# Attention in eight places per pair: a head group's last turn and products of values moved into the next pair

## What is computed

```python
proj = h @ w_in
# A: 8 query heads over 2 key/value heads, head_dim 64, dense; q and k RMS-normalised, 2-D rotary
s = jnp.einsum('bqgrd,bkgd->bgrqk', q_blk, k)
p = jax.nn.softmax(s, axis=-1)
a_o = jnp.einsum('bgrqk,bkgd->bqgrd', p, v)
# B: three groups of 8 heads, (window, dilation) = (128,1), (512,4), (2048,16), partial rotary
o, lse = _dilated_group(_partial_rope(b_q, pos) * scale, _partial_rope(b_k, pos), b_v, window, dilation)
wts = jax.nn.softmax(jnp.stack(lses, axis=0), axis=0)
b_o = jnp.einsum('gbsh,gbshd->bshd', wts, jnp.stack(outs, axis=0))
x = x + jnp.concatenate([a_o, b_o], axis=-1) @ w_out
# then: RMSNorm -> SwiGLU FFN -> residual; the second layer's mixer is a gated recurrence
```

## Time and profile before

| | us |
|---|---|
| median of 3 runs | 1305.33 |
| lowest, highest | 1304.08, 1308.48 |
| profiled execution, its own time | 1305.52 |
| its span in the trace | 1303.7 |

### The profile page before, as it was taken

How to read it: one execution, slowest core, us unless ns; L and a number is a source line. 1 busy time by engine, 2 the same in 40 slices (tenths; PEclk the granted TensorE clock), 3 DMA queues, 4 the chain that set the end, 5 groups by cost and what they waited for, 6 DMA issues and landing times.

```text
span 1303.7 us, 18386 instructions
## 1 busy us (share of the span) xinstructions
PE 1285.2 (99%) x6525; PEld 1030.1 (79%) x6525; DVE 560.3 (43%) x872; ACT 551.6 (42%) x1006; POOL 611.3 (47%) x487
## 2 busy tenths in 40 slices
PE   8999999999999999999999999999999999999998
PEld 7877777777778888888888876777888888888886
DVE  4866575756644512222202026999843131311011
ACT  5454444444434433333323246786433333333233
POOL 4565564646535444444444543530244444444442
PEclk9999999999999999999999999999999999999999
DMA  6422222222314333333332353214333333333332
GB/s 217 150 73 62 68 64 59 57 66 67 120 56 115 91 97 97 97 97 97 98 97 88 105 166 117 81 57 145 91 97 96 98 95 98 96 116 98 96 98 94
DMA packets 123415, 126.31 MB, mean 97 GB/s; under 512 B 7896, under 2 KB 106456, under 8 KB 122712
## 3 DMA queue, kind: packets, MB, share of 16 engines
q1 hardware_dynamic: 123320, 125.46, 32.1%
q10 hardware_dynamic: 32, 0.01, 0.0%
HBM read 119.15 MB, written 6.29 MB: 96 GB/s over the span
## 4 chain that ended last, share of the span: by engine, by line
PE 58%; issue 21%; POOL 12%; DVE 5%; ACT 3%; POOLq 0%; DMA 0%; SPq 0%; ACTq 0%; DVEq 0%
PE ps L1495 17%; PE ps L1497 16%; PE ps L1496 16%; POOL w_lo L495 11%; PE ps L1855 2%; PE ps L1613 1%; PE ps L1648 1%; PE ps L1625 1%; PE ps L1629 1%; PE ps L1590 1%; POOL rot L504 1%; PE ps L1659 1%; PE ps L1667 1%; DVE bkn L1139 1%; ACT w_hi L555 0%
## 5 line engine op out<-in xcount | busy, mean ns | idle before, releaser
L495 POOL TENSOR_TENSOR w_lo<-w_stage,w_hi 128x512 fp32r<-128x512 f32 (+2 forms) x430 | 543.3, 1268 | 676.8 <-ACT w_hi L555 676.4
L555 ACT ACTIVATE w_hi<-w_stage 128x512 fp32r<-128x512 f32 (+2 forms) x448 | 264.0, 594 | 582.4 <-PE ps L1497 570.0
L1495 PE MATMUL ps<-h_hi,w_hi 128*128 128x512 f32 x1104 | 439.7, 398 | 1.8 <-DVE h_lo L950 1.2
L1497 PE MATMUL ps<-h_hi,w_lo 128*128 128x512 f32 x1104 | 430.2, 390 | 0.0
L1496 PE MATMUL ps<-h_lo,w_hi 128*128 128x512 f32 x1104 | 430.1, 390 | 0.0
L1495 PEld LDWEIGHTS ps<-h_hi,w_hi 128*128 128x128 f32 x1104 | 207.3, 188 | 63.7 <-issue 17.0
L1497 PEld LDWEIGHTS ps<-h_hi,w_lo 128*128 128x128 f32 x1104 | 207.3, 188 | 43.6
L1496 PEld LDWEIGHTS ps<-h_lo,w_hi 128*128 128x128 f32 x1104 | 207.5, 188 | 43.1 <-issue 2.6
L1278 DVE TENSOR_TENSOR silu_g<-ps,rstd_wide 128x512 f32<-128x512 f32 x44 | 30.2, 686 | 327.4 <-PE ps L1497 327.4
L1495 PE MATMUL ps<-w_hi,f_hi 128*128 128x512 f32 x176 | 68.6, 390 | 0.1
L1496 PE MATMUL ps<-w_lo,f_hi 128*128 128x512 f32 x176 | 68.5, 389 | 0.0
(11 more groups left out here) (229 smaller groups left out, 1637.7 us busy)
## 6 DMA issues: line engine op xcount, KB each, us to landing
w_stage<-in_ffn_w_gate_up_dram SPq DMA_DIRECT2D x176, 256.0 KB, 3.1
w_stage<-in_ffn_w_down_dram SPq DMA_DIRECT2D x88, 256.0 KB, 2.7
w_stage<-in_even_w_in_dram SPq DMA_DIRECT2D x96, 192.0 KB, 2.5
w_stage<-in_odd_w_in_dram SPq DMA_DIRECT2D x32, 256.0 KB, 2.8
x_spill<-x_t SPq DMA_DIRECT2D x2, 2048.0 KB, 8.5
x_t<-x_spill SPq DMA_DIRECT2D x2, 2048.0 KB, 7.9
w_stage<-in_odd_w_out_dram SPq DMA_DIRECT2D x16, 256.0 KB, 2.7
w_stage<-in_even_w_out_dram SPq DMA_DIRECT2D x16, 192.0 KB, 2.4
```

The source lines that it names most:

```text
L495: pool.tensor_tensor(out=w_lo[:, s, 0:n], in0=stage[:, s, 0:n], in1=w_hi[:, s, 0:n].bitcast(f32), op=ALU.subtract).then_inc(chunk_lo, 1)
L555: act.activation(w_hi[:, j % RING, 0:n], stage[:, j % RING, 0:n], ACT.Copy).then_inc(chunk_hi, 1)
L1495: pe.matmul(out_, lh, rh, start=start, stop=False, skip_group_check=skip)
L1497: return pe.matmul(out_, ll, rh, start=False, stop=stop, skip_group_check=skip)
```

## The change

The four steps of A in pair p had scores at j = 10, 13, 16, 19 and turns at 13, 16, 19, 22. Now the scores are at 10, 13, 16, 20, the turns at 13, 16, 20, and the fourth turn is at j = 0 of the next pair, ahead of B's first scores. A's products of values go from j = 0 to j = 2 of the next pair (also in the output projection), ahead of `v_turn`, and their split to the chunk after. B's fourth turn goes from j = 12 to 13, ahead of A's first turn, and B's products from 13 to 16, their split from 14 to 17. Places are now j = 0, 2, 5, 8, 10, 13, 16 and 20. No instruction is added or dropped. The numbers in `turns_before_*` are unchanged, as the order among the turns is.

```diff
-A_TURN = {13: 0, 16: 1, 19: 2, 22: 3}
+A_TURN = {13: 0, 16: 1, 20: 2}
...
-A_OUT, B_VALUES, B_OUT, LAST_OUT = 1, 13, 14, 8
+A_VALUES = (None, 2, 2, 2, 1)
+A_OUT, B_VALUES, B_OUT, LAST_OUT = (None, 3, 3, 3, 2), 16, 17, 8
...
 def a_turn_at(p, j):
 
-    return None if p == 4 else A_TURN.get(j)
+    if j == 0 and p:
+        return p - 1, 3
+    return (p, A_TURN[j]) if p < 4 and j in A_TURN else None
...
                 if j == 0 and p:
+                    a_turn(p - 1, 3)
                     b_scores(p - 1, 0)
+                if j == A_VALUES[p]:
                     a_values(p - 1)
                 if j == V_TURN[p]:
                     v_turn(p - 1)
...
-                if at_ is not None:
-                    a_turn(p, at_)
+                if at_ is not None and j:
+                    a_turn(*at_)
```

More of the change, by code:

```diff
@@ L85, in width @@
     return 512
-A_SCORES = {10: 0, 13: 1, 16: 2, 19: 3}
-A_TURN = {13: 0, 16: 1, 19: 2, 22: 3}
+A_SCORES = {10: 0, 13: 1, 16: 2, 20: 3}
+A_TURN = {13: 0, 16: 1, 20: 2}
 B_SCORES = {0: 0, 2: 1, 5: 2, 8: 3}
-B_TURN = {5: 0, 8: 1, 10: 2, 12: 3}
+B_TURN = {5: 0, 8: 1, 10: 2, 13: 3}
 LAST_SCORES = {0: 0, 1: 1, 2: 2, 4: 3}
@@ L772, in attention @@
                     b_turned(p - 1, b)
-                if (c := a_turn_at(p, j)) is not None:
-                    if p == 0 and c == 0:
+                if (turn := a_turn_at(p, j)) is not None:
+                    if turn == (0, 0):
                         act.wait_ge(spilled, 16)
-                    a_turned(p, c)
+                    a_turned(*turn)
                 if (b := b_scores_at(p, j)) is not None:
@@ L780, in attention @@
                     a_exps(p, c)
-                if p and j == A_OUT:
+                if j == A_OUT[p]:
                     out_hi(2 * p - 2, p - 1)
@@ L1172, in attention @@
                 if at_ is not None:
-                    if p == 0 and at_ == 0:
+                    if at_ == (0, 0):
                         dve.wait_ge(spilled, 16)
-                    a_turned(p, at_)
+                    a_turned(*at_)
                 if bs is not None:
```

## The result

The changed kernel takes 1312.49 us (median of 6 runs, 1311.77 to 1313.68), the kernel before 1305.37 on the same chip (6 runs). The ratio is 1.0055, 95% interval 1.0042 to 1.0067: slower by 7.1 us, where 3.8 were forecast and the range ended at 1311.8. The profiled execution took 1311.78 us with a span of 1309.9, 6.2 us more than the 1303.7 before.

The account below looks back on a forecast made before the run. TensorE, busy for 99% of the span, was taken as the bound. Stalls +6.15, A's products apart +0.6 and vanished waits -2.9 gave +3.8 us: 1309.1 us forecast (+0.29%), range 1305.8 to 1311.8.

Parts of the forecast that it names:

- The stall: A's first turn, j = 13, pairs 1 to 3: waits 2.05 us for copies queued behind VectorE's addition; +6.15 us.
- The rival in which VectorE comes first: At j = 12 VectorE's addition starts before GpSimd's subtraction, 0.69 us for 1.45: +1.5 us, 1306.8; chance 0.12.
- A's products apart: A's products of values moved from j = 0 to 2: extra switches, 0.15 us in four places, +0.6 us.
- The waits that vanish: Waits at A's third turn (0.68) and for `bkn` at the pair's end (0.28) go in pairs 0 to 2: -2.9 us.
- The other rivals: Bare stall 1306.1 (chance 0.06), no stall 1303.0 (0.05), late value banks 1313.1 (0.08), late `x_t` refill 1311.7 (0.04).
- wait for `vf` or `bvn` at a pair's first chunk: Pair's start: value banks free too late, 4 x 1.0 us on top at 2 us late, 1313.1; chance 0.08.
- late weights in the output stage: Output stage: refill of `x_t` holds up the weights, 2.6 us more at 5 us late, 1311.7; chance 0.04.

Follow-up runs that it names:

- The undone turn: Changed kernel with B's last turn back at j = 12, all else of the change kept: 1304.09 us, ratio 0.9987.
- the copies put first: Changed kernel with VectorE's addition of j = 12 done at j = 13 in pairs 1 to 3, behind the copies of both turns: 1307.55 us, ratio 1.0019.
- The early rotation: A's query rotation moved from j = 15 of the pair before to j = 3 of its own: changed kernel 1311.68 us; kernel before 1304.42, again 1301.28.
- the products taken back to j = 13: Changed kernel with B's last turn back at j = 12 and B's products back at j = 13: 1305.16 us, ratio 0.9999.
- the run with the products in it: Changed kernel with eight unused 512-column products on TensorE ahead of A's first turn in pairs 1 to 3: 1310.06 us, ratio 1.0038.

## Why the prediction was wrong

**The stall: right, in place, cause and size.** 2.05 us were forecast in each of pairs 1 to 3; the traces have 2.07 (2.96 less the estimated 0.88). The addition took 1.47 (forecast 1.45) and was blocked by the subtraction that GpSimd had begun 0.07 us earlier. The undone turn and the copies put first show both halves of it. The rival in which VectorE comes first didn't occur: in all 12 stalls of the four traces that have them the addition took 1.46 to 1.49. The Trainium skill (SBUF — State Buffer, "SBUF: two separate sides") gives the shared ports to whoever starts first; the traces agree, with GpSimd first by 0.06 to 0.08 us each time. The rows show why that order was steady: the addition is released by the end of GpSimd's product (156.50), and the subtraction is the next thing in GpSimd's own queue. I had given the rival 0.12 for two starts 0.1 us apart and hadn't asked what sets their order. Elsewhere the other order does occur: in pair 0 of the kernel before another addition of VectorE began at 87.61 and took 0.68, and GpSimd's product, begun at 87.63, took 1.82, where the shortest of its size there took 1.27.

**A's products apart: right in the whole, with a part mis-sized.** 0.15 were forecast for each place. The output stage has +0.16. Measured alone it is 0.27, and A's fourth turn at the pair's start, which I had priced at nothing, gives 0.12 back. That the two come out at 0.15 together is luck.

**The waits that vanish: this step failed for pair 0.** The prediction took "0.98 for each of the three pairs" from the difference of pairs 1 and 3, and didn't look at VectorE in pair 0. There are no B products at j = 16 of pair 0, and so VectorE gets no room behind the query rotation of j = 15; with the fourth turn at the pair's end it is `bkn` that is late, by 1.15 us in place of 0.2. The early rotation removes that wait, and in pairs 1 and 2 the products taken back to j = 13 bring one of 0.56. In pairs 1 and 2 the step held. It cost 0.87 us by the table, 0.68 without TensorE's later arrival.

**What no step had: the clock behind the stall.** The row first: after 1.92 us of idle TensorE the eight transposes and four scores took 3.68 us in place of 2.03, at a granted clock of 1.2 GHz for 3.4 us. That is 1.6 us, and it happened at one of three stalls in the first trace, another one in the second, and two of three in the third (the changed kernel with the early rotation). The Trainium skill (TensorE: Matmul & The Clock Gate, "Part 1: The HAM clock gate") says that a monitor that runs freely sets the clock by how busy TensorE has been lately. The traces agree with the part that can be seen: the same idle time at the same place of the program is followed by a fall in one execution and by none in another. The step that failed is the stall's price: I took its length alone, 3 x 2.05, and put what a stall does to the clock at nothing. Per stall it was 4 falls in 9, so by my estimate about 0.7 us on the average, some 2 us for three stalls. That the stall brings the falls is borne out by the run with the products in it; that they come here by chance and not by something else that varies between executions isn't shown.

**What stays open.** The table explains the profiled execution, 6.3 us over the one before (1311.78 less 1305.52), with a fall of the clock behind its end in either execution. The medians are 7.1 apart, since the execution profiled was the second lowest of its six. Which of the six had how many falls isn't known, because only a profiled one shows where they are; all six have a mean clock of 0.997 or less.

The other rivals did not come: no wait for `vf` or `bvn` at a pair's first chunk, and no late weights in the output stage, where TensorE's idle times are those of before (0.89 ahead of B's products and 1.89 behind the wait for `o_lo`, for 0.90 and 1.88).

## What to carry to other kernels

When a change closes a gap between two users of the same buffers, look first at what the queue that frees them does at that moment; here one table entry was worth 7.5 us, more than everything else in the change. Ask also which instruction releases each of two engines that want the same thing: that tells which comes first. Before restructuring to hide a wait, ask what makes the engine late: moving one block of VectorE's work by twelve chunks removed the waits with TensorE's order untouched, and by the windows beat the reordering (75.57 us a pair for 75.72). And check every stretch to which a measured saving is applied: the first pair of a software pipeline lacks the steps that belong to the pair before it, and with them their cover.

## What the runs showed of the hardware

- TensorE's granted clock fell for 3.4 us at 1.2 GHz behind idle times of 1.9 us and more, in some executions and not in others. In the 13 traces read here (both kernels and all experiments), the places were: A's first turn, idle 1.9, 4 of 9; the output projection behind the wait for `o_lo`, idle 1.9, 6 of 13; the recurrent stage, idle 2.7, 6 of 13. The three filled stalls had none, and neither had any of 35 shorter waits in the same traces: 0.89 to 0.90 ahead of B's products of the output stage (13), 0.90 in the run with the copies first (3), 1.12 to 1.15 at the end of pair 0 (6), 0.97 to 1.25 behind `h_lo` at 13 to 15 us (13). From 13 us of the span on, no trace has a wait between 1.25 and 1.9 us.
- One fall costs about 1.6 us here, and two separate the two groups of runs of one and the same program (medians 1301.7 and 1305.2). For differences of 0.2% in this kernel the windows of a trace tell more than ten runs do.
- An addition of two operands that lie in SBUF took 1.46 to 1.49 us when a subtraction on GpSimd had begun just before it, in 12 of 12 stalls, against 0.69 alone. Copies out of PSUM of half that size took 0.41 to 0.43 while GpSimd worked.
- 16 transposes through the same two banks, with ScalarE and VectorE both free, need 2.93 us in place of an estimated 1.88 (1.93 and 0.88 to the start of the second eight, 1.0 for these): emptying the banks between them costs 1.05.
